# Before the first layer: small loads from GpSimd's queue, and the first modulation summed by VectorE and four small matmuls

## What is computed

```
c_act = silu(c)                                   # 1024 numbers
mod = c_act @ ada_w[l] + ada_b[l]                 # 1024 x 6144 matrix, six pieces of 1024
sh1, sc1, g1, sh2, sc2, g2 = split(mod, 6)
h = rmsnorm(x, norm1_g[l]) * (1 + sc1) + sh1
proj = h @ w_in[l]
```

## Time and profile before

| | us |
|---|---|
| median of 3 runs | 2326.13 |
| lowest and highest | 2325.88, 2326.4 |
| the profiled execution's own time | 2329.56 |
| its span in the trace | 2327.1 |
| TensorE busy | 2264.4 (97%) |
| VectorE busy | 1628.7 (70%) |
| ScalarE busy | 1098.3 (47%) |
| GpSimd busy | 1008.1 (43%) |

### The profile page before, as it was taken

One profiled execution on the slowest core, in us unless ns is written; L12 is line 12 of the kernel. 1 busy time (PEld: TensorE's weight loads), 2 busy tenths in 40 slices (PEclk: granted clock), 3 DMA queues, 4 the chain that ended last, 5 costly groups with the idle time before them and its releaser, 6 DMA issues.

```text
span 2327.1 us, 30806 instructions
## 1 busy us (share of the span) xinstructions
PE 2264.4 (97%) x11289; PEld 1833.2 (79%) x11289; DVE 1628.7 (70%) x2095; ACT 1098.3 (47%) x1808; POOL 1008.1 (43%) x641
## 2 busy tenths in 40 slices
PE   6999999999899999999999999999989999999998
PEld 5888866787788888888878787668878888888887
DVE  6885458449876666777888744672796767677886
ACT  4345546434444444444543464662444444444455
POOL 1222377444987777300012124043389777760000
PEclk7999999999999999999999999999999999999999
DMA  8742323342333333487557131004313333347763
GB/s 292 281 151 62 88 64 110 109 127 73 93 116 96 117 98 117 149 286 253 153 215 245 55 81 51 1 30 171 118 55 113 113 91 114 91 131 259 257 208 113
DMA packets 273012, 311.08 MB, mean 134 GB/s; under 512 B 37033, under 2 KB 191647, under 8 KB 271839
## 3 DMA queue, kind: packets, MB, share of 16 engines
q1 hardware_dynamic: 272174, 307.94, 40.7%
q10 hardware_dynamic: 688, 1.18, 0.2%
HBM read 246.53 MB, written 61.49 MB: 132 GB/s over the span
## 4 chain that ended last, share of the span: by engine, by line
PE 85%; DVE 7%; issue 2%; ACT 2%; POOL 1%; DMA 0%; DVEq 0%; SPq 0%; ACTq 0%; POOLq 0%
PE bank L1497 31%; PE bank L1067 18%; PE bank L1512 17%; PE bank L1127 6%; PE bank L1328 2%; PE bank L1360 1%; PE bank L1288 1%; DVE hLo L2150 1%; PE bank L1388 1%; DVE xT L2144 1%; PE bank L1217 1%; DVE xT L2472 1%; DVE tLo L2541 1%; ACT swaProb L1872 1%; PE bank L1195 1%
## 5 line engine op out<-in xcount | busy, mean ns | idle before, releaser
L987 POOL TENSOR_TENSOR wLo<-raw,wHi 128x1024 fp32r<-128x1024 f32 x66 | 161.5, 2448 | 411.4 <-ACT wHi L989 411.4
L1690 POOL TENSOR_TENSOR prodLo<-comb,prodHi 128x512 fp32r<-128x512 f32 x160 | 234.0, 1470 | 122.0 <-ACT prodHi L1029 122.0
L1497 PE MATMUL bank<-tHi,prodHi 128*128 128x512 f32 x640 | 249.9, 390 | 5.7 <-DVE tLo L2541 4.2
L1497 PE MATMUL bank<-tLo,prodHi 128*128 128x512 f32 x640 | 249.1, 389 | 0.0
L1497 PE MATMUL bank<-tHi,prodLo 128*128 128x512 f32 x640 | 249.1, 389 | 0.0
L1512 PE MATMUL bank<-gateHi,downHi 128*128 128x512 f32 x616 | 240.3, 390 | 0.0
L1512 PE MATMUL bank<-gateHi,downLo 128*128 128x512 f32 x616 | 239.7, 389 | 0.0
L1512 PE MATMUL bank<-gateLo,downHi 128*128 128x512 f32 x616 | 239.7, 389 | 0.0
L1029 ACT ACTIVATE prodHi<-comb 128x512 fp32r<-128x512 f32 x160 | 100.9, 634 | 249.0 <-PE bank L1497 228.7
L2486 DVE SCALAR_TENSOR_TENSOR ub<-bank,ffp,ub 128x1023 f32<-128x1023 f32 x88 | 112.8, 1282 | 141.9 <-ACT ub L1958 140.3
L1497 PE MATMUL bank<-hHi,prodHi 128*128 128x512 f32 x480 | 187.1, 390 | 7.1 <-POOL prodLo L1690 4.5
(11 more groups left out here) (393 smaller groups left out, 5346.4 us busy)
## 6 DMA issues: line engine op xcount, KB each, us to landing
raw<-in_ffn_w_up_dram SPq DMA_DIRECT2D x88, 512.0 KB, 4.8
gateRaw<-gateOut SPq DMA_DIRECT2D x154, 256.0 KB, 4.2
adaE<-in_ada_w_dram SPq DMA_DIRECT2D x64, 512.0 KB, 6.5
gateOut<-gateSums SPq DMA_DIRECT2D x22, 1024.0 KB, 5.5
raw<-in_w_in_dram SPq DMA_DIRECT2D x34, 512.0 KB, 4.1
downRaw<-in_ffn_w_down_dram SPq DMA_DIRECT2D x66, 256.0 KB, 3.8
raw<-in_w_out_dram SPq DMA_DIRECT2D x28, 512.0 KB, 3.8
downCols<-in_ffn_w_down_dram SPq DMA_DIRECT2D x24, 512.0 KB, 3.6
```

The source lines that it names most:

```text
L987: eng.tensor_tensor(lo[:], raw[slot][:], fview(hi[:]), ALU.subtract).then_inc(s["split_lo"], 1)
L1497: last = mm(o, w[idx][:, c0], moving(idx, kp, hi), start=kp == 0 and q_ == 0, stop=kp == 3 and q_ == 2)
L1690: pool.tensor_tensor(sLoW[idx][:], product_source(js, idx), fview(sHiW[idx][:]), ALU.subtract).then_inc(s["us_lo"], 1)
```

## The change

1. Positions, the sixteen parameter loads and the five loads of the first two weight tiles are issued by GpSimd, after it has made its masks and before it waits for the rounded weight tiles. SP issues c, the rotary constants, x and then all sixteen adaw tiles in a row. The new loads have semaphores of their own that are never cleared.
2. `ADA_GROUP` becomes tiles 0-2, 3-5, 6-8, 9-11, 12-13, 14 and 15.
3. VectorE accumulates tiles 1-7 into adas 0 and 8-14 into adas 1, and folds each sum itself into foldFirst. TensorE multiplies tiles 0 and 15 by c_act, and four small matmuls with quadSum take the place of the two sums by a column of ones. Three small VectorE operations take the place of five.
4. In the layers, the six semaphores of the adaE loads become two; the waits ask for the same loads.

```diff
-ADA_GROUP = [0, 0, 1, 1, 2, 2, 3, 3, 4, 4, 4, 5, 5, 5, 6, 6]
+ADA_GROUP = [0, 0, 0, 1, 1, 1, 2, 2, 2, 3, 3, 3, 4, 4, 5, 6]
...
-                sp.dma_start(posi[64:128, :], positions.to_broadcast([64, T])).then_inc(s["small_loaded"], 16)
...
-                for i in range(8):
+                for i in range(2 * KT):
                     load_adaw(i)
-                load_params(sp, lambda w: w[0:1], prow)
-                for i in range(8, 2 * KT):
-                    load_adaw(i)
-                for n in range(AHEAD):
-                    load_win(sp, w_in[0:1], n, n, s[f"next_loaded{n}"])
...
+                pool.dma_start(posi[64:128, :], positions.to_broadcast([64, T])).then_inc(s["pos_loaded"], 16)
+                load_params(pool, lambda w: w[0:1], prow)
+                for n in range(AHEAD):
+                    load_win(pool, w_in[0:1], n, n, s[f"next_loaded{n}"])
                 for n in range(AHEAD):
                     split_ahead(pool, n)
...
                 pe.wait_ge(s["c_act"], 1)
-                for g in range(2):
-                    pe.wait_ge(s[f"ada_loaded{ADA_GROUP[g * KT]}"], 16 * ADA_GROUP.count(ADA_GROUP[g * KT]))
-                    part_sums(adaw[g * KT], (2 + g) * KT, cact[:, 0:1])
-                pe.wait_ge(s["ada_done"], KT - 1)
-                part_sums(adas[0], 0, caus01[:, P - 1:P])
+                ada_tile(0, 2 * KT)
                 spread_rms(pe, "n1")
-                pe.wait_ge(s["ada_done"], 2 * KT - 2)
-                part_sums(adas[1], HALF, caus01[:, P - 1:P])
+                ada_tile(2 * KT - 1, 3 * KT)
+                pe.wait_ge(s["ada_done"], 2 * KT)
+                for r in range(4):
+                    last = pe.matmul(bank[0][32 * r:32 * r + 32, 0:2 * KT], quad[:], foldP[:].rearrange("p j c -> p (j c)")[:, r:2 * 32:4],
+                                     start=True, stop=True)
+                last.then_inc(s["ada_sum"], 1)
...
-                for n, i in enumerate([i for i in range(2 * KT) if i % KT]):
+                for i in range(1, 2 * KT - 1):
...
+                    if i in (KT - 1, 2 * KT - 2):
+                        dve.wait_ge(s["ada_done"], KT * g + KT - 1)
+                        link(dve.transpose(nt[2][:], adas[g][:]))
+                        dve.tensor_reduce(foldP[:, g, :], nt[2][:].rearrange("p (c i) -> p c i", i=32), AX.X, ALU.add).then_inc(s["ada_done"], 1)
-                    if i == KT + 2:
+                    if i == KT + 4:
...
-                    if i == KT + 1:
+                    if i == KT + 3:
...
+                dve.wait_ge(s["ada_sum"], 2)
+                dve.wait_ge(s["params_copied"], 1)
+                link(dve.tensor_tensor(mod[:, 0:2 * KT], bank[3][:, 16 + 2 * KT:16 + 4 * KT], prm[:, R_ADAB:R_ADAB + 2 * KT], ALU.add))
                 dve.wait_ge(s["ada_sum"], 3)
-                link(dve.tensor_copy(mod[:, 0:2 * KT], bank[3][:, 16 + 2 * KT:16 + 4 * KT]))
-                link(dve.tensor_tensor(mod[:, 0:KT], mod[:, 0:KT], bank[3][:, 16:16 + KT], ALU.add))
-                dve.wait_ge(s["ada_sum"], 4)
-                link(dve.tensor_tensor(mod[:, KT:2 * KT], mod[:, KT:2 * KT], bank[3][:, 16 + HALF:16 + HALF + KT], ALU.add))
-                first_modulation(dve)
+                link(dve.tensor_tensor(mod[:, 0:2 * KT], mod[:, 0:2 * KT], bank[0][:, 0:2 * KT], ALU.add))
+                dve.scalar_tensor_tensor(out=scl[:, 0, :], in0=mod[:, KT:2 * KT], scalar=1.0, in1=prm[:, R_N1:R_N1 + KT],
+                                         op0=ALU.add, op1=ALU.mult).then_inc(s["mod_first"], 1)
```

More of the change, by code:

```diff
@@ L466, in build @@
     adaw = [place(f"adaw{i}", [P, D], F32, at["h"] + 4 * K * i) for i in range(2 * KT)]
-    adas = [place(f"adas{g}", [P, D], F32, E[(12, 13, 15)[g]]) for g in range(3)]
+    adas = [place(f"adas{g}", [P, D], F32, E[12 + g]) for g in range(2)]
+    foldP = place("foldFirst", [P, 2, 32], F32, E[15])
     two_pi = 6.283185307179586
@@ L475, in build @@
     parts.append(float(np.float32(rest)))
+    held = ExitStack()
+    by_pool = sems(held, ["first_pos", "first_params", "first_win0", "first_win1"])
     with ExitStack() as st:
@@ L555, in part_sums, with ada_tile @@
                     last.then_inc(s["ada_sum"], 1)
+                def ada_tile(i, column):
+                    pe.wait_ge(s[f"ada_loaded{ADA_GROUP[i]}"], 16 * ADA_GROUP.count(ADA_GROUP[i]))
+                    part_sums(adaw[i], column, cact[:, i % KT:i % KT + 1])
                 pe.wait_ge(s["c_act"], 1)
[L558 to L565 removed]
+                ada_tile(0, 2 * KT)
+                spread_rms(pe, "n1")
+                ada_tile(2 * KT - 1, 3 * KT)
[4 more added lines that the diff above has]
+                last.then_inc(s["ada_sum"], 1)
             def copy_x(eng, t, sem):
@@ L648, in _ @@
             def _(sp):
-                for name in sorted(s)[0::5]:
+                for name in cleared[0::5]:
                     sp.sem_clear(s[name])
@@ L653, in _ @@
             def _(pool):
-                for name in sorted(s)[1::5]:
+                for name in cleared[1::5]:
                     pool.sem_clear(s[name])
@@ L658, in _ @@
             def _(act):
-                for name in sorted(s)[2::5]:
+                for name in cleared[2::5]:
                     act.sem_clear(s[name])
@@ L663, in _ @@
             def _(dve):
-                for name in sorted(s)[3::5]:
+                for name in cleared[3::5]:
                     dve.sem_clear(s[name])
@@ L2179, in step_sizes, with early_products @@
                 dve.tensor_tensor_scan(dcum, n0, n1, 0.0, ALU.mult, ALU.add).then_inc(s["dt_ready"], 1)
-            def early_products(j, ks, n, landed):
-                dve.wait_ge(s[f"ada_early_loaded{n}"], nth(f"ada_early_loaded{n}", 16 * landed))
+            def early_products(j, ks, n):
+                dve.wait_ge(s[f"ada_early_loaded{n % 2}"], nth(f"ada_early_loaded{n % 2}", 16 * (KT + 4 * (n // 2))))
                 acc = nt[2 + j % 2]
@@ L2238, in key_rope @@
                     rope(dve.tensor_tensor(misc[a, :], misc[a, :], misc[b, :], ALU.add), 3)
-            early_products(0, range(KT), 0, KT)
+            early_products(0, range(KT), 0)
             step_sum()
@@ L2243, in _ @@
             mod_fold(0)
-            early_products(1, range(KT), 1, KT)
+            early_products(1, range(KT), 1)
             mod_fold(1)
@@ L2268, in _ @@
                 if j == 0:
-                    early_products(2, range(4), 2, 4)
+                    early_products(2, range(4), 2)
                 if j == 1:
@@ L2272, in _ @@
                 if j == 2:
-                    early_products(2, range(4, KT), 3, 4)
+                    early_products(2, range(4, KT), 3)
                 if j == 3:
                     mod_fold(2)
-                    early_products(3, range(2), 4, 4)
+                    early_products(3, range(2), 4)
                 if j == 4:
-                    early_products(3, range(2, 4), 4, 4)
+                    early_products(3, range(2, 4), 4)
                 if j == 5:
-                    early_products(3, range(4, KT), 5, 4)
+                    early_products(3, range(4, KT), 5)
                     mod_fold(3)
```

25 lines of the change are left out of this document (15 added, 10 removed), and 3 rows, old and new, of the table PER_LAYER.

## The result

| | before | changed |
|---|---|---|
| median of 9 runs each, us | 2326.48 | 2335.05 |
| lowest and highest | 2324.41, 2331.75 | 2330.40, 2337.07 |
| the profiled execution's own time | 2329.56 | 2335.69 |
| its span in the trace | 2327.1 | 2333.9 |
| first matmul of the first layer | 51.61 | 60.24 |

The ratio is 1.0028, 95% interval [1.0017, 1.0039], which is 4 to 9 us: the change makes the kernel slower, and the measured time lies above the predicted range (2323.8 to 2330.5).

A forecast was written before the change was run, and what follows sets the result against it. It took the opening, bounded by VectorE's own work after 23.6, to move the TensorE-bound rest one for one: - 1.3 (VectorE's list) + 1.7 (collision) = + 0.4 us, so 2326.5 us as median, range 2323.8 to 2330.5.

The forecast's parts named there:

- What bounds the kernel: Whole kernel: TensorE busy 97% of the span; what the opening saves or loses moves the rest one for one.
- When tiles land: Adaw loads: 1.27 us a tile, parameters 2.3, weight tiles 5.1; tile 5 at 23.6 if GpSimd's loads take nothing.
- Rival 3: Opening: moved loads all go ahead, tile 14 at 42.4, tile 15 at 43.7; + 0.6 us, 2326.7; chance 0.10.
- VectorE's list: Opening: products, turns and sums without a wait after 23.6, ending at 46.5 against 47.80, a gain of 1.3 us.
- TensorE's list: Opening: tile 15's 3.57 us of matmuls end at about 43.6, before VectorE's sum at 45.4, costing nothing.
- GpSimd's list: Opening: 22 loads at 1 us each, last issued at 25.6, landing about 4.1 later; weight tiles there between 13 and 43.
- Rival 4: Opening: GpSimd's issue ends last; at 2.0 us an issue the second weight tile lands at 51.7, + 7.4, 2333.5; chance 0.08.
- The collision: Opening: a GpSimd subtraction beside products costs VectorE 1.7 us; one of two taken so, + 1.7.
- rival 2: Opening: both GpSimd subtractions fall beside products, + 3.4 us, 2328.2; chance 0.25.
- Rival 5: Opening: VectorE's angle passes held by GpSimd's issuing, 8.5 us, of which 5.0 on the path; 2331.5; chance 0.07.
- the signs that I had named: Opening trace: if right, scl ready between 46.5 and 49.9 and VectorE without a wait for adaw after about 24.

The follow-up runs named there:

- the fold alone: The change without moving the loads: SP issues all in before's order; 2326.66 against 2326.27 us, ratio 1.0001, first matmul 52.71.
- the kernel with the same place and the other queue: The change with SP issuing all loads, parameters and weight tiles between x and adaw, GpSimd none; 2333.78 against 2326.68 us, ratio 1.0031.
- the kernel with the queue alone: Before's computation in the opening, with the 22 loads issued by GpSimd; 2330.14 against 2326.27 us, ratio 1.0020, first matmul 57.94.

## Why the prediction was wrong

**What bounds the kernel** held within what the times can tell: the layers follow the opening. The first matmul came 8.63 later and the median 8.6. That the two agree so closely is luck, since the ratio, 1.0028, is 6.5 us and its interval 4 to 9, and six of the experiments gave back 0.7 to 3.5 us behind the first matmul. So "one for one" is not shown to the microsecond.

**When tiles land** is the step that failed. Its prices were right (2.3 and 5.1 predicted, 2.13 and 4.99 measured). So was the pace: with SP's order the second group came at 23.53 for 23.6. Wrong was which of its two cases I took. I let what GpSimd issues take nothing from SP's tiles, although the issue that I assumed, 1 us a load, already puts all 22 among x and adaw. The runs showed the other case in its place: the second group at 30.65 and not 23.6, 7.12 us later than with SP's order, and every later product behind it. (The Trainium skill, "DMA: Bandwidth & Descriptors", section "Issuing engines are not separate DMA queues", has the DMAs that different engines start run on the same 16 DMA engines and interleave, and the kernel with SP as the issuer agrees: 30.70 against 30.65.)

**Rival 3** had the right mechanism, all moved loads ahead, and the wrong bill. I applied the 7.4 us only to tiles 14 and 15, and asked whether they would still arrive before they are wanted. But the list of VectorE hangs on the second group: with that 7.4 later, everything behind it is 7.4 later. The same sum with 23.6 + 7.4, and with both subtractions beside the products, is - 1.3 + 7.4 + 3.4 = + 9.5 us, against 8.6 measured. Instead I gave it + 0.6 and a chance of 0.10.

**VectorE's list** was right. From 23.6 to the last product I had 42.9 - 23.6 = 19.3 us; measured are 52.70 - 30.65 = 22.05, less 3.0 of collision 19.05. It never waited for a tile behind the second group. "Its own work is the bound" was the sentence that should have warned me: a list without a wait has no slack in which a late start could be lost.

**TensorE's list** was right: tile 15's matmuls ended at 53.18 (49.77 + 3.41), before the second sum at 55.24, and the small matmuls took 0.31.

**GpSimd's list**: 0.5 to 1 us an issue for my 1, landing 5.4 to 9.1 for my 4.1; the second weight tile was rounded by 30.5, as early as the case I named. Rival 4, the slow issue, fell.

**The collision** was right in size and wrong in number: I took one subtraction beside products, it was both, 3.0 us together where rival 2 had 3.4.

**Rival 5**, the held angles, was there in small: four one-input passes took 0.94 instead of 0.69 to 0.75 while GpSimd issued the pieces of the weight tiles.

```profile
13.49 0.94 DVE L617 TENSOR_SCALAR nt<-nt,ropec 64x1024 f32<-64x1024 f32 x1
14.47 0.94 DVE L619 TENSOR_SCALAR nt<-nt,ropec 64x1024 f32<-64x1024 f32 x1
```

The larger delay was in their start: I had put it 1.9 us later, and it was 7.02 (12.35 for 5.33), since the positions took 8.7 us to land. Still, the angles ended at 23.89, and VectorE then waited 2.97 for tile 1: no cost.

Of the signs that I had named, scl came at 56.11 and not between 46.5 and 49.9, and the last wait for adaw ended at 30.65 and not at 24.

The account from the experiments: the fold alone starts its layer at 50.37, the change at 57.89, 7.52 later. The lateness adds 7.12 and the collision 3.0. The wait for the third group that the fold alone had (1.53) is gone, and so is the hold of scl (1.12). Together 7.47.

## What to carry to other kernels

Moving a load to another engine's queue doesn't take it out of the way; it moves it to another place in the same stream. So write down when the first consumer gets its data, not only the last one. When a list of work has no wait left behind some load, the lateness of that load is the lateness of the end: price a change of transfer order there first. And a rival whose mechanism is likely deserves the full sum again, step by step, not a correction at its end.

## What the runs showed of the hardware

- The gap from GpSimd's last instruction to the next block grew with the loads that it had issued: 1.83, 1.92, 3.24 and 3.64 us for 0, 1, 17 and 22, although these had landed long before. It is paid only when GpSimd is last. What is done in that time no row shows.
- A load issued by GpSimd among full queues landed late: 8.7 us for the positions, 5.4 to 7.1 for parameter rows of 0.5 to 44 KB, 7.2 to 9.1 for the weight pieces, with the DMA engines at a share of 1.0. SP's x tiles took longer beside them too (9.8 us for 7.2 in before), and the positions took 3.4 when SP issued them ahead of x. VectorE's first operation moved from 5.33 to 12.35 by this and by the later issue (3.56 for 1.68).
- Up to 45 us the trace has the same 14.07 MB as 9520 packets when SP issues all (the kernel with the same place and the other queue) and as 4545 when GpSimd issues the 22. The second group came at 30.70 and 30.65 all the same.
- Beside GpSimd's issues of the weight pieces, four of VectorE's one-input passes took 0.2 to 0.25 us longer each; the cast before them, beside the first of these issues, did not (0.69), and none did where GpSimd had no such pieces to issue. (The Trainium skill, "SBUF — State Buffer", section "Who interferes with whom", has a VectorE operation in a two-port mode, which a tensor_scalar can enter, and a GpSimd one block each other for the whole instruction. Here an issue took about 1 us and the passes lost less, with no hole between them; whether they ran in such a mode no row shows.)
- A GpSimd subtraction beside two-input products cost VectorE 1.5 to 2.0 us: 3.0 for two in the change, where the first had begun 1.04 us before the products, 4.04 for two in the kernel with the queue alone, 1.9 for one with the weight tiles by SP.
- The TensorE clock was granted at 0.50 (1.2 GHz) in the last windows of both openings, whether TensorE had been busy with one-column matmuls (5.00 of 5 us in the windows from 30 to 40 of before) or nearly idle (0.45 and 0.00 us in the same windows of the change). The first 96 matmuls took 24.81 us in both: a start 8.6 us later cost no clock.
